# One sparse-expert layer: the products of 96-row expert jobs, alternating or in two sweeps

## The chip, the cores and the metric

The kernel runs on one core of one Trainium2 chip. The metric is the device time of one execution, in microseconds. The kernel before took 2451.39 us (median of 3 runs, 2450.69 to 2453.16).

## The reference

One layer of a diffusion backbone over 1024 latent tokens of width 1024: a mixer (a recurrent scan and a gated linear attention), a layer norm, and a mixture of experts. Only the last matters here. All in float32:

```
logits = h @ w_router + b_router            # 1024 tokens, 32 experts
top_v, top_i = top_k(logits, 4); top_w = softmax(top_v)
for the tokens xb of expert e:
    gate = min(xb @ w_gate[e] + b_gate[e], 7)
    up   = clip(xb @ w_up[e] + b_up[e], -7, 7)
    act  = (up + 1) * gate * sigmoid(1.702 * gate)
    y    = act @ w_down[e] + b_down[e]      # times the token's weight, added to its row
x = layer_norm(alpha * x + g2 * sum of y)
```

Each of the three weight matrices of an expert is 1024 x 1024 float32, 4 MB.

## The kernel before, in words

From about 797 us to 2400 us of the span the kernel works through a table of expert jobs, made on the chip. A job has one expert and at most 128 tokens. There are four kinds: 4 is full (128 rows), 3 has 96 rows, 2 has 64 rows, 1 has 32 rows. In a full job the tokens are the stationary operand of TensorE (128 columns) and the weights stream past, 512 at a time. A job of 64 rows uses half of the array's columns for each product, so two products (j = 0, 1), each over another 512 of the weight columns, lie in the two halves of the array: the "half products". A job of 32 rows has four products of 256 columns in the four quarters: the "quarter products". A job of 96 rows does both, 64 rows as half products and 32 rows as quarter products, from the same weights.

One iteration of the job loop on TensorE (in the `block.tensor` body) does, in this order: the gate and up products of job u for the first four k tiles (`gate_up(..., 0, KD // 2)`), the transposes of the activations of job u-1 (`turn`), the gate and up products for the other four k tiles, the transposes of the gathered tokens of job u+1, and the down products of job u-1 over all eight k tiles (`down`). I call these three blocks of products sections. Each section uses eight 128 x 1024 weight tiles, two in each piece: in `gate_up` k tile by k tile, first gate (g = 0), then up (g = 1); in `down` k tile by k tile. In a job of 96 rows each such tile gets two half products and then four quarter products (lines 567 to 575, and 592 to 602), so that they alternate.

Weights lie in a ring of twelve pieces of 1 MB, `ring[q]`: eight for gate and up (two k tiles each), four for down. Each has one buffer. The last product that reads a piece raises `gu_used` or `dn_used`; SyncE waits on it (`gu_pieces` at line 479, `dn_pieces` at line 507), and then issues the load of the next expert's piece into the same place. TensorE waits for a piece (`d_gu[q]`, `d_dn[q]`) before its first product with it. SyncE's queue is in order: in one iteration the eight gate and up pieces of job u+1, the two bias rows (line 513, after `gu_free`, which VectorE raises when it has read the gate and up products out of PSUM), the four down pieces of job u, and the down bias (line 509). Loads are only issued for the first job of an expert.

After the second gate/up section VectorE reads PSUM (lines 1625 and 1628) and computes the activation with ScalarE; after a down section it adds the bias and the token's weight (lines 1609, 1614), and GpSimd adds the rows to the result in DRAM with indirect DMAs (line 1758; in a job of 96 rows two, one after the other). GpSimd also gathers the tokens of later jobs (line 1745).

Of the kernel before, what the change touches and what calls it, by code (L numbers as in the profile page):

```python
# [20 lines left out]
P = 128  # L21
BANK = 512
# [15 lines left out]
def layer(nc, x, c, ctx, c_ctx, w_ada, b_ada, w_in, conv_w, conv_b, lru_wa, lru_ba, lru_wx, lru_bx,  # L38
# [7 lines left out]
    KD = D // P  # L46
# [13 lines left out]
    HT, QR = 64, 32  # L60
    QW = D // 4
# [5 lines left out]
    GUP, DNP = 8, 4  # L67
# [12 lines left out]
    with ctxs:  # L80
# [3 lines left out]
        def sem(name):  # L84
            return ctxs.enter_context(nc.semaphore(name))
# [21 lines left out]
        def reg(off, *shape):  # L107
            n = 1
            for s in shape:
                n *= s  # L110
            assert off + n <= AW
            v = arena[:, off:off + n]
            if len(shape) == 2:
                v = v.rearrange("p (a b) -> p a b", a=shape[0])
            if len(shape) == 3:
                v = v.rearrange("p (a b c) -> p a b c", a=shape[0], b=shape[1])
            if len(shape) == 4:
                v = v.rearrange("p (a b c d) -> p a b c d", a=shape[0], b=shape[1], c=shape[2])
            return v
# [104 lines left out]
        ring = [reg(2048 * q, 2, D) for q in range(GUP + DNP)]  # L224
        o = O_X1 + 8192
        xg = reg(o, D); o += 1024
        xT = reg(o, KD, P); o += 1024
# [3 lines left out]
        aT = reg(o, KD, P); o += 1024  # L231
# [10 lines left out]
        ps = [psall[:, i * BANK:(i + 1) * BANK] for i in range(8)]  # L242
# [7 lines left out]
        QUARTER_AT = {1: P - QR, 3: HT - QR}  # L250
# [40 lines left out]
        d_gu = [sem(f"d_gu{q}") for q in range(GUP)]  # L291
        d_dn = [sem(f"d_dn{q}") for q in range(DNP)]
        d_bias, d_bdn = sem("d_bias"), sem("d_bdn")
        gu_used, dn_used, gu_free = sem("gu_used"), sem("dn_used"), sem("gu_free")
# [85 lines left out]
        def settle(eng):  # L380

            eng.sem_inc(settled[eng.engine], 1)
# [167 lines left out]
        def gate_up(pe, kind, u, order_, k0, k1):  # L550
            if k0 == 0:
                pe.wait_ge(xT_ready, u + 1)
                pe.wait_ge(gu_free, u + 1)
            for k in range(k0, k1):
                for g in range(2):
                    q = 2 * (k // 2) + g
                    if k % 2 == 0:
                        pe.wait_ge(d_gu[q], order_)
                        if kind < 4:
                            settle(pe)  # L560
                    w = ring[q][:, k % 2]
                    if kind == 4:
                        for s in range(2):
                            mm = pe.matmul(ps[2 * g + s], xT[:, k, :], w[:, s * BANK:(s + 1) * BANK],  # L564
                                           start=(k == 0), stop=(k == KD - 1))
                    if kind in (2, 3):
                        for j in range(2):
                            mm = pe.matmul(ps[2 * g][HT * j:HT * j + HT, :], xT[:, k, HT:P], w[:, j * BANK:(j + 1) * BANK],  # L568
                                           start=(k == 0), stop=(k == KD - 1), skip_group_check=True)
                    if kind in (1, 3):  # L570
                        r = slice(QUARTER_AT[kind], QUARTER_AT[kind] + QR)
                        for j in range(4):
                            mm = pe.matmul(ps[2 * g + 1][QR * j:QR * j + QR, 0:QW], xT[:, k, r], w[:, j * QW:(j + 1) * QW],  # L573
                                           start=(k == 0), stop=(k == KD - 1), skip_group_check=True)
                    if k % 2:
                        mm.then_inc(gu_used, 1)

        def down(pe, kind, u, order_):
            pe.wait_ge(aT_act, u + 1)
            pe.wait_ge(aT_dve, u + 1)  # L580
            pe.wait_ge(y_biased, u + 1)
            for k in range(KD):
                if k % 2 == 0:
                    pe.wait_ge(d_dn[k // 2], order_)
                    if kind < 4:
                        settle(pe)
                w = ring[GUP + k // 2][:, k % 2]
                if kind == 4:
                    for s in range(2):
                        mm = pe.matmul(ps[6 + s], aT[:, k, :], w[:, s * BANK:(s + 1) * BANK],  # L590
                                       start=(k == 0), stop=(k == KD - 1))
                if kind in (2, 3):
                    for j in range(2):
                        mm = pe.matmul(ps[6][HT * j:HT * j + HT, :], aT[:, k % 4, HT * (k // 4):HT * (k // 4) + HT],  # L594
                                       w[:, j * BANK:(j + 1) * BANK],
                                       start=(k == 0), stop=(k == KD - 1), skip_group_check=True)
                if kind in (1, 3):
                    for j in range(4):
                        mm = pe.matmul(ps[7][QR * j:QR * j + QR, 0:QW], aT[:, 4 + k % 2, QR * (k // 2):QR * (k // 2) + QR],  # L599
                                       w[:, j * QW:(j + 1) * QW],  # L600
                                       start=(k == 0), stop=(k == KD - 1), skip_group_check=True)
                if k % 2:
                    mm.then_inc(dn_used, 1)

        def by_kind(eng, t, what):
            with eng.If(t > 2):
# [28 lines left out]
        def _(pe):  # L635
# [281 lines left out]
            with pe.Fori(0, OUTER) as o4:  # L917
                with pe.If(typ_of(pe, typ_p) + typ_of(pe, typ_c) > 0):
                    with pe.Fori(0, INNER) as i4:
                        u = o4 * INNER + i4  # L920
                        t, on_ = typ_of(pe, typ_c), ord_of(pe, ord_c, wait_c)
                        by_kind(pe, t, lambda kind: gate_up(pe, kind, u, on_, 0, KD // 2))
                        tp, op_ = typ_of(pe, typ_p), ord_of(pe, ord_p, wait_p)
                        with pe.If(tp > 0):
                            pe.wait_ge(act_ready, u + 1)
                            pe.wait_ge(xT_ready, u + 1)
                            by_kind(pe, tp, lambda kind: turn(pe, ub, JOB_KINDS[kind][2] // P, JOB_KINDS[kind][1] // P).then_inc(act_turned, 1))
                            pe.nop()
                        by_kind(pe, t, lambda kind: gate_up(pe, kind, u, on_, KD // 2, KD))
                        job_row(pe, [typ_n, ord_n], u + 2)  # L930
                        with pe.If(typ_of(pe, typ_n) > 0):
                            pe.wait_ge(xg_ready, u * 16 + 32)
                            pe.wait_ge(aT_act, u + 1)
                            pe.wait_ge(aT_dve, u + 1)
                            turn(pe, xg, KD).then_inc(x_swapped, 1)
                        by_kind(pe, tp, lambda kind: down(pe, kind, u, op_))
                        for to, of in ((typ_p, typ_c), (ord_p, ord_c), (typ_c, typ_n), (ord_c, ord_n)):
                            pe.reg_mov(to, of)
                    pe.nop()
# [892 lines left out]
```

## Time and profile before

| | |
|---|---|
| median of 3 runs | 2451.39 us |
| span of the profiled execution | 2448.2 us |
| what lies around that span, taken as the median less the span | 3.2 us |
| TensorE matmul busy | 2266.8 us, 93% of the span |
| VectorE, ScalarE, GpSimd busy | 931.4, 564.2, 230.1 us |
| DMA over the span | 567.22 MB, mean 232 GB/s |

The profiled execution has no time of its own beside its span; what is around the span is small and the same for both kernels, as far as is known. A busy TensorE is one with a matmul in flight. A group of the timeline is a run of like instructions: its start, its length until its last instruction ends, engine, line, operation and tile, and in brackets the idle time ahead of it with what ended it. TensorE's instructions overlap a little, so the true length of a group is the distance to the start of the next one. A float32 matmul of the program shows as two records.

### The profile page before, as it was taken

How to read it: one execution, taken by the hardware profiler on the slowest of the kernel's cores; microseconds unless marked ns; L12 is line 12 of the kernel's file. 1: busy time of each engine (PE TensorE's matmuls, PEld its weight loads, DVE VectorE, ACT ScalarE, POOL GpSimd, SP SyncE). 2: the span in 40 equal slices, each digit the busy share in tenths (PEclk: the TensorE clock that was granted, in tenths of full speed). 3: DMA queues.
4: the chain of work that ended last, by engine and by line, in shares of the span. 5: the costliest groups of instructions: out<-in, count | busy, mean ns of one | idle time of the engine just before them, and what ended most of it. 6: DMA issues, size and time to landing. Idle time of an engine off the chain costs nothing.

```text
span 2448.2 us, 32313 instructions
## 1 busy us (share of the span) xinstructions
PE 2266.8 (93%) x10269; PEld 1016.2 (42%) x10270; DVE 931.4 (38%) x1493; ACT 564.2 (23%) x676; POOL 230.1 (9%) x259
## 2 busy tenths in 40 slices
PE   6889999789949999999998899999999999999992
PEld 3444444554534334343442333344333444444441
DVE  2665742656661332333224232323143222222234
ACT  2333443521111122222112121212112212112113
POOL 0000000002310010010100001100001010000000
PEclk8989999889969999999999999999999999999996
DMA  9222310022245877899489999858999658997744
GB/s 332 66 79 66 101 49 26 1 85 99 95 170 210 291 275 237 299 354 380 154 306 409 375 385 404 294 176 261 342 365 397 233 175 315 311 364 265 235 122 165
DMA packets 182739, 567.22 MB, mean 232 GB/s; under 512 B 16140, under 2 KB 51136, under 8 KB 181546
## 3 DMA queue, kind: packets, MB, share of 16 engines
q1 hardware_dynamic: 167434, 524.19, 57.7%
q0 software_dynamic: 15264, 42.48, 7.1%
q8 instruction: 26, 0.43, 0.1%
q14 instruction: 15, 0.12, 0.0%
HBM read 537.26 MB, written 31.46 MB: 232 GB/s over the span
## 4 chain that ended last, share of the span: by engine, by line
PE 86%; DVE 6%; DMA 4%; SPq 1%; ACT 1%; issue 1%; POOL 0%; DVEq 0%; POOLq 0%; ACTq 0%
PE psall L564 26%; PE psall L590 13%; PE psall L568 10%; PE psall L733 10%; PE psall L573 5%; PE psall L594 5%; PE psall L631 3%; PE psall L721 3%; PE psall L844 2%; PE psall L838 2%; PE psall L599 2%; DMA arena<-in_w_down_dram 2%; PE psall L700 1%; DMA arena<-in_x_dram 1%; DVE arena L1342 1%
## 5 line engine op out<-in xcount | busy, mean ns | idle before, releaser
L564 PE MATMUL psall<-arena 128*128 128x512 f32 x1472 | 643.2, 595 | 6.8 <-DVEq L1649 3.1
L564 PEld LDWEIGHTS psall<-arena 128*128 128x128 f32 x1472 | 277.9, 191 | 350.4 <-issue 348.5
L590 PE MATMUL psall<-arena 128*128 128x512 f32 x736 | 321.8, 595 | 3.6 <-DVE arena L1662 3.6
L568 PE MATMUL psall<-arena 128*64 128x512 f32 x1152 | 280.7, 605 | 7.5 <-DMA arena<-in_w_up_dram 5.3
L1625 DVE TENSOR_TENSOR arena<-psall,arena 32x256 f32<-32x256 f32 (+2 forms) x123 | 79.9, 649 | 508.0 <-PE psall L564 321.5
L733 PE MATMUL psall<-arena 128*128 128x512 f32 (+1 forms) x608 | 246.6, 563 | 0.7 <-ACT arena L957 0.7
L1133 ACT COPY arena<-psall 128x512 f32<-128x512 f32 x49 | 28.7, 586 | 837.8 <-PE psall L631 837.8
L590 PEld LDWEIGHTS psall<-arena 128*128 128x128 f32 x736 | 138.8, 191 | 170.1 <-issue 170.1
L1609 DVE TENSOR_TENSOR arena<-psall,arena 32x256 f32<-32x256 f32 (+2 forms) x123 | 79.8, 649 | 300.6 <-PE psall L590 202.4
L1662 DVE COPY arena<-psall 128x512 f32<-128x512 f32 x49 | 33.9, 691 | 353.7 <-PE psall L631 353.6
L733 PEld LDWEIGHTS psall<-arena 128*128 128x128 f32 x608 | 116.5, 192 | 120.7 <-issue 116.4
L1136 ACT COPY arena<-psall 128x1024 f32<-128x1024 f32 x48 | 48.6, 1013 | 482.4 <-PE psall L631 482.4
L594 PE MATMUL psall<-arena 128*64 128x512 f32 x576 | 142.7, 612 | 10.8 <-DMA arena<-in_w_down_dram 10.8
L573 PE MATMUL psall<-arena 128*32 128x256 f32 x2048 | 140.3, 386 | 0.3 <-issue 0.2
L568 PEld LDWEIGHTS psall<-arena 128*64 128x64 f32 x1152 | 70.8, 136 | 148.1 <-issue 148.1
L573 PEld LDWEIGHTS psall<-arena 128*32 128x32 f32 x2048 | 52.7, 109 | 129.3 <-issue 110.8
L631 PE MATMUL psall<-ident,arena 128*128 128x128 f32 x680 | 94.0, 279 | 11.3 <-DMA arena<-h_rows,lruw 5.1
L631 PEld LDWEIGHTS psall<-ident,arena 128*128 128x128 f32 x680 | 76.8, 142 | 64.9 <-issue 59.5
L1758 POOL DMA_INDIRECT stream_rows<-arena,lruw x57 | 90.3, 1584 | 92.8 <-DMA stream_rows<-arena,lruw 45.8
L1614 DVE SCALAR_TENSOR_TENSOR arena<-arena,lruw,adarow 32x256 f32<-32x256 f32 (+2 forms) x123 | 87.0, 707 | 6.7
L1742 POOL COPY lruw<-lruw 128x1 int32 (+1 forms) x49 | 9.2, 188 | 771.8 <-PE psall L631 725.9
L1628 DVE SCALAR_TENSOR_TENSOR arena<-psall,arena 32x256 f32<-32x256 f32 (+2 forms) x123 | 79.6, 647 | 1.8
(281 smaller groups left out, 1968.2 us busy)
## 6 DMA issues: line engine op xcount, KB each, us to landing
arena<-in_w_gate_dram SPq DMA_DIRECT2D x128, 1024.0 KB, 7.1
arena<-in_w_up_dram SPq DMA_DIRECT2D x128, 1024.0 KB, 8.4
arena<-in_w_down_dram SPq DMA_DIRECT2D x128, 1024.0 KB, 7.9
arena<-in_w_ada_dram SPq DMA_DIRECT2D x16, 1024.0 KB, 5.3
arena<-in_b_gate_dram SPq DMA_DIRECT2D x32, 512.0 KB, 7.4
arena<-in_b_up_dram SPq DMA_DIRECT2D x32, 512.0 KB, 8.5
arena<-in_b_down_dram SPq DMA_DIRECT2D x32, 512.0 KB, 7.5
arena<-in_w_ada_dram SPq DMA_DIRECT2D x4, 2048.0 KB, 14.5
```

The lines of the kernel that those rows point to most:

```text
L564: mm = pe.matmul(ps[2 * g + s], xT[:, k, :], w[:, s * BANK:(s + 1) * BANK], start=(k == 0), stop=(k == KD - 1))
L568: mm = pe.matmul(ps[2 * g][HT * j:HT * j + HT, :], xT[:, k, HT:P], w[:, j * BANK:(j + 1) * BANK], start=(k == 0), stop=(k == KD - 1), skip ...
L573: mm = pe.matmul(ps[2 * g + 1][QR * j:QR * j + QR, 0:QW], xT[:, k, r], w[:, j * QW:(j + 1) * QW], start=(k == 0), stop=(k == KD - 1), skip ...
L590: mm = pe.matmul(ps[6 + s], aT[:, k, :], w[:, s * BANK:(s + 1) * BANK], start=(k == 0), stop=(k == KD - 1))
L594: mm = pe.matmul(ps[6][HT * j:HT * j + HT, :], aT[:, k % 4, HT * (k // 4):HT * (k // 4) + HT], w[:, j * BANK:(j + 1) * BANK], start=(k == ...
L631: mm = pe.transpose(psT[:, k * P:(k + 1) * P], src[:, k * P:(k + 1) * P], ident[:, :])
L733: mm = pe.matmul(ps[i % JB][0:w, 0:seg[1] - seg[0]], wring[n % WRING][:, k, 0:w], uT[:, k, seg[0]:seg[1]], start=(k == 0), stop=(k == KD - 1))
L1609: mm = dve.tensor_tensor(yb[p0:p1, c:c + n], psY[p0:p1, c:c + n], ebias[p0:p1, 2, b:b + n], ALU.add)
L1614: mm = dve.scalar_tensor_tensor(out=yb[p0:p1, c:c + n], in0=yb[p0:p1, c:c + n], scalar=(wcolq if c else wcol)[p0:p1], in1=adarow[p0:p1, 3, ...
L1625: mm = dve.tensor_tensor(gb[p0:p1, c:c + n], psG[p0:p1, c:c + n], ebias[p0:p1, 0, b:b + n], ALU.add)
L1628: mm = dve.scalar_tensor_tensor(out=ub[p0:p1, c:c + n], in0=psU[p0:p1, c:c + n], scalar=1.0, in1=ebias[p0:p1, 1, b:b + n], op0=ALU.add, op ...
L1758: return pool.indirect_dma_start(out=to, out_offset=bass.IndirectOffsetOnAxis(ap=index, axis=0), in_=yb[:, cols], in_offset=None, bounds_c ...
```

## The change

In both `gate_up` and `down` the loop over weight tiles is put inside a loop over "sweeps". A job of 96 rows has two sweeps: first all half products of the section (eight tiles, in four pieces), then all quarter products of the same tiles. Other kinds have one sweep, which is the loop as it was. The waits for pieces stand in the first sweep, the release of a piece in the last.

```diff
-            for k in range(k0, k1):
-                for g in range(2):
-                    q = 2 * (k // 2) + g
-                    if k % 2 == 0:
-                        pe.wait_ge(d_gu[q], order_)
...
-                    if kind in (2, 3):
-                        for j in range(2):
-                            mm = pe.matmul(ps[2 * g][HT * j:HT * j + HT, :], xT[:, k, HT:P], w[:, j * BANK:(j + 1) * BANK],
-                                           start=(k == 0), stop=(k == KD - 1), skip_group_check=True)
-                    if kind in (1, 3):
-                        r = slice(QUARTER_AT[kind], QUARTER_AT[kind] + QR)
-                        for j in range(4):
...
-                    if k % 2:
-                        mm.then_inc(gu_used, 1)
+            sweeps = {4: ("full",), 3: ("half", "quarter"), 2: ("half",), 1: ("quarter",)}[kind]
+            for sweep in sweeps:
+                for k in range(k0, k1):
+                    for g in range(2):
+                        q = 2 * (k // 2) + g
+                        if k % 2 == 0 and sweep == sweeps[0]:
+                            pe.wait_ge(d_gu[q], order_)
+                            if kind < 4:
+                                settle(pe)
+                        w = ring[q][:, k % 2]
...
+                        if sweep == "half":
+                            for j in range(2):
+                                mm = pe.matmul(ps[2 * g][HT * j:HT * j + HT, :], xT[:, k, HT:P], w[:, j * BANK:(j + 1) * BANK],
+                                               start=(k == 0), stop=(k == KD - 1), skip_group_check=True)
+                        if sweep == "quarter":
+                            r = slice(QUARTER_AT[kind], QUARTER_AT[kind] + QR)
+                            for j in range(4):
...
+                        if k % 2 and sweep == sweeps[-1]:
+                            mm.then_inc(gu_used, 1)
```

`down` is changed in the same way, over its eight k tiles, with `d_dn` and `dn_used`.

## Rows read from the trace of the kernel before

**Rows 1.** The page: the chain that ended last, by line.

```profile
PE psall L564 26%; PE psall L590 13%; PE psall L568 10%; PE psall L733 10%; PE psall L573 5%; PE psall L594 5%; PE psall L631 3%; PE psall L721 3%; PE psall L844 2%; PE psall L838 2%; PE psall L599 2%; DMA arena<-in_w_down_dram 2%; PE psall L700 1%; DMA arena<-in_x_dram 1%; DVE arena L1342 1%
```

**Rows 2.** Groups of instructions, page and by form: count, busy us, mean ns, idle before.

```profile
L1133 ACT COPY arena<-psall 128x512 f32<-128x512 f32 x49 | 28.7, 586 | 837.8 <-PE psall L631 837.8
...
L564 PE MATMUL psall<-arena 128*128 128x512 f32 x1472 | 643.2, 595 | 6.8 <-DVEq L1649 3.1 <-issue 1.9 <-DVE arena L1628 1.7
L568 PE MATMUL psall<-arena 128*64 128x512 f32 x1152 | 280.7, 605 | 7.5 <-DMA arena<-in_w_up_dram 5.3 <-DVE arena L1628 1.9
L573 PE MATMUL psall<-arena 128*32 128x256 f32 x2048 | 140.3, 386 | 0.3 <-issue 0.2
```

**Rows 3.** TensorE's timeline, one gate/up section of a 96-row job, start and end.

```profile
810.33 1.08 PE L568 MATMUL psall<-arena 128*64 128x512 f32 x4
811.34 0.64 PE L573 MATMUL psall<-arena 128*32 128x256 f32 x8
811.91 1.08 PE L568 MATMUL psall<-arena 128*64 128x512 f32 x4
...
822.96 1.09 PE L631 MATMUL psall<-ident,arena 128*128 128x128 f32 x8
```

**Rows 4.** TensorE's timeline where a 64-row section precedes a 32-row section.

```profile
2321.76 7.09 PE L594 MATMUL psall<-arena 128*64 128x512 f32 x32
2328.77 3.66 PE L573 MATMUL psall<-arena 128*32 128x256 f32 x64
2332.37 1.09 PE L631 MATMUL psall<-ident,arena 128*128 128x128 f32 x8
```

**Rows 5.** TensorE's waits from 797 to 2400 us: total us, times, longest.

```profile
PE psall L594 <- DMA arena<-in_w_down_dram: 10.8, 7, 2.6
PE psall L568 <- DMA arena<-in_w_up_dram: 5.3, 4, 1.7
```

**Rows 6.** Stretches: us, engines' busy us (records), TensorE clock, DMA share, GB/s.

```profile
1107.00:1170.00 63.00, 63.00 (x412) 18.29 (x412) 20.79 (x34) 13.01 (x12) 5.94 (x8) 1.00 0.98 374
1251.00:1371.00 120.00, 104.99 (x690) 36.85 (x682) 39.76 (x74) 26.02 (x24) 13.57 (x18) 1.00 1.02 394
1408.00:1563.00 155.00, 153.06 (x930) 55.59 (x918) 51.07 (x88) 30.74 (x29) 16.70 (x22) 1.00 1.01 391
1823.00:1880.00 57.00, 53.64 (x410) 19.38 (x410) 28.12 (x56) 14.25 (x13) 8.29 (x11) 0.97 1.01 389
```

**Rows 7.** Line 507 at 1142 to 1145 us: issues (first, last), us to landing.

```profile
L507 SPq DMA_DIRECT2D arena<-in_w_down_dram x4: 372/378/384, 1142.4 to 1144.3; - x4
...
DMA to landing us min/median/max: 7.3/9.2/14.1
```

**Rows 8.** The same of line 507 at 1310 to 1311 us.

```profile
L507 SPq DMA_DIRECT2D arena<-in_w_down_dram x2: 2162/2234/2305, 1307.9 to 1310.4; - x2
...
DMA to landing us min/median/max: 20.2/20.2/20.2
```

**Rows 9.** The same of line 507 at 1544 to 1545 us.

```profile
L507 SPq DMA_DIRECT2D arena<-in_w_down_dram x1: 373/373/373, 1544.4 to 1544.4; - x1
...
DMA to landing us min/median/max: 18.0/18.0/18.0
```

**Rows 10.** The same of line 479 at 1816 to 1819 us.

```profile
L479 SPq DMA_DIRECT2D arena<-in_w_gate_dram x1: 373/373/373, 1816.8 to 1816.8; - x1
...
DMA to landing us min/median/max: 5.4/6.2/6.9
```

**Rows 11.** TensorE's timeline: starts of three 96-row down sections, end of a 64-row one.

```profile
1156.93 1.08 PE L594 MATMUL psall<-arena 128*64 128x512 f32 x4
...
1321.80 1.08 PE L594 MATMUL psall<-arena 128*64 128x512 f32 x4 [1.95 <-DMA arena<-in_w_down_dram]
...
1368.24 1.94 PE L594 MATMUL psall<-arena 128*64 128x512 f32 x8 [0.58 <-DMA arena<-in_w_down_dram]
...
1560.01 1.08 PE L594 MATMUL psall<-arena 128*64 128x512 f32 x4
```

More of the change, by code:

```diff
@@ L553, in gate_up @@
                 pe.wait_ge(gu_free, u + 1)
-            for k in range(k0, k1):
-                for g in range(2):
-                    q = 2 * (k // 2) + g
-                    if k % 2 == 0:
-                        pe.wait_ge(d_gu[q], order_)
[L559 to L565, printed above, removed]
-                    if kind in (2, 3):
-                        for j in range(2):
-                            mm = pe.matmul(ps[2 * g][HT * j:HT * j + HT, :], xT[:, k, HT:P], w[:, j * BANK:(j + 1) * BANK],
-                                           start=(k == 0), stop=(k == KD - 1), skip_group_check=True)
-                    if kind in (1, 3):
-                        r = slice(QUARTER_AT[kind], QUARTER_AT[kind] + QR)
-                        for j in range(4):
-                            mm = pe.matmul(ps[2 * g + 1][QR * j:QR * j + QR, 0:QW], xT[:, k, r], w[:, j * QW:(j + 1) * QW],
-                                           start=(k == 0), stop=(k == KD - 1), skip_group_check=True)
-                    if k % 2:
-                        mm.then_inc(gu_used, 1)
@@ new lines, in gate_up @@
+            sweeps = {4: ("full",), 3: ("half", "quarter"), 2: ("half",), 1: ("quarter",)}[kind]
[8 more added lines that the diff above has]
+                        w = ring[q][:, k % 2]
+                        if sweep == "full":
+                            for s in range(2):
+                                mm = pe.matmul(ps[2 * g + s], xT[:, k, :], w[:, s * BANK:(s + 1) * BANK],
+                                               start=(k == 0), stop=(k == KD - 1))
+                        if sweep == "half":
[5 more added lines that the diff above has]
+                            for j in range(4):
+                                mm = pe.matmul(ps[2 * g + 1][QR * j:QR * j + QR, 0:QW], xT[:, k, r], w[:, j * QW:(j + 1) * QW],
+                                               start=(k == 0), stop=(k == KD - 1), skip_group_check=True)
+                        if k % 2 and sweep == sweeps[-1]:
+                            mm.then_inc(gu_used, 1)
@@ L581, in down @@
             pe.wait_ge(y_biased, u + 1)
[L582 to L603, printed above, removed]
@@ new lines, in down @@
+            sweeps = {4: ("full",), 3: ("half", "quarter"), 2: ("half",), 1: ("quarter",)}[kind]
+            for sweep in sweeps:
+                for k in range(KD):
+                    if k % 2 == 0 and sweep == sweeps[0]:
+                        pe.wait_ge(d_dn[k // 2], order_)
+                        if kind < 4:
+                            settle(pe)
+                    w = ring[GUP + k // 2][:, k % 2]
+                    if sweep == "full":
+                        for s in range(2):
+                            mm = pe.matmul(ps[6 + s], aT[:, k, :], w[:, s * BANK:(s + 1) * BANK],
+                                           start=(k == 0), stop=(k == KD - 1))
+                    if sweep == "half":
+                        for j in range(2):
+                            mm = pe.matmul(ps[6][HT * j:HT * j + HT, :], aT[:, k % 4, HT * (k // 4):HT * (k // 4) + HT],
+                                           w[:, j * BANK:(j + 1) * BANK],
+                                           start=(k == 0), stop=(k == KD - 1), skip_group_check=True)
+                    if sweep == "quarter":
+                        for j in range(4):
+                            mm = pe.matmul(ps[7][QR * j:QR * j + QR, 0:QW], aT[:, 4 + k % 2, QR * (k // 2):QR * (k // 2) + QR],
+                                           w[:, j * QW:(j + 1) * QW],
+                                           start=(k == 0), stop=(k == KD - 1), skip_group_check=True)
+                    if k % 2 and sweep == sweeps[-1]:
+                        mm.then_inc(dn_used, 1)
```

## The prediction

> **What bounds the kernel now.** I read the chain that ended last first. Nearly all of it is TensorE, and its matmuls lead line by line: the half products of lines 568 and 594 have 15% of the span, the quarter products of lines 573 and 599 have 7% [rows 1]. DMA has a small share, loads of w_down. So a shorter section of TensorE shortens the kernel, except where a weight load sets the pace. Next I read TensorE's waits in the expert stage: it waited for w_down seven times, 10.8 us in all, and for w_up four times, 5.3 us [rows 5]. That is 16 us in 1603 us, which looks like nothing. But a wait shows only where weights already come late. The third view, busy time by stretch, shows how near the others are: in four stretches that hold 96-row jobs the DMA engines are 98 to 102% busy [rows 6]. In these the loads have just enough time, and a faster TensorE can run into them. The reader is to see both: TensorE is the bound by its busy time, with a second bound close behind it in those stretches.
>
> **How many jobs and sections.** ScalarE's copy at line 1133 is run once per job, so there are 49 jobs [rows 2]. A full job has 64 gate/up records (8 k tiles, 2 matrices, 2 column blocks, 2 records each): 1472/64 = 23 full jobs. Half records: 64 per job, 1152/64 = 18 jobs of kinds 2 and 3. Quarter records: 128 per job, 2048/128 = 16 jobs of kinds 1 and 3. As 49 - 23 = 26 jobs hold halves or quarters, 18 + 16 - 26 = 8 have both. So the change touches 8 jobs of 96 rows, with 3 sections each: 24 sections. Their first gate/up sections start at about 810, 981, 1107, 1271, 1429, 1503, 1751 and 1792 us, their down sections at 867, 1032, 1157, 1322, 1490, 1560, 1819 and 1848.
>
> **What one section costs before.** A half group starts at 810.33, its quarter group at 811.34, the next half group at 811.91: 1.01 + 0.57 = 1.58 us for one weight tile. Eight of them end at 822.96: 12.63 us for the section [rows 3]. All 24 have this pattern and, within 0.2 us, this length.
>
> **What it costs after.** The two sweeps are what jobs of other kinds do already. A section of half products alone, with a quarter section behind it, takes 2328.77 - 2321.76 = 7.01 us; the quarter section, with transposes behind it, 2332.37 - 2328.77 = 3.60 us [rows 4]. Both include the changes of pattern at their ends that the new section has. Sum 10.61 us. Saved: 12.63 - 10.61 = 2.02 us per section, and 24 x 2.02 = 48.5 us if nothing else binds. The number of products, their sizes and their operands stay, so what goes is 14 of the 16 changes between halves and quarters, 2.02/14 = 0.144 us each. As rows of both patterns are there, this term has narrow ends: 1.8 to 2.1 us per section.
>
> What the trace shows here is a loss at every change of tile width. The Trainium skill ("TensorEngine Tiling (Array Packing)", Key Properties) says that changing the tiling mode drains the engine, and "TensorE: Matmul & The Clock Gate" (Step-by-step: what each phase is for) gives a drain of about 128 cycles. At 2.4 GHz this is an estimate of 0.053 us per change, 0.75 us per section and 18 us in all, against 0.144 us by the rows. I go by the rows, which are of this very work.
>
> **The waits and releases that move.** A section's four pieces were needed at 0, 1.6, 6.3 and 7.9 us (gate/up) or 0, 3.2, 6.3 and 9.5 us (down) from its start. With 7.01/8 = 0.88 us per tile in the first sweep they are needed at 0, 0.9, 3.5, 4.4 or 0, 1.75, 3.5, 5.3. Behind a late last piece come, in a down section, two tiles of halves and all quarters: 1.75 + 3.60 = 5.35 us, where it was 2 x 1.58 = 3.16. Pieces are given back in the second sweep only. For the first piece of a gate/up section that is at 7.01 + 3 x 0.45 = 8.4 us, not at 4.7; the last is given back at the section's end, 2 us earlier than before. Behind the wait on TensorE stand only TensorE's own products; behind the later release stand SyncE's loads. Where the DMA engines have a backlog, a later issue costs nothing: the loads issued at 1142.4 to 1144.3 landed up to 14.1 us later, the one at 1310.4 20.2 us later, against 5.4 us for one issued into idle engines at 1816.8 [rows 7, 8, 10]. Where they have none, the piece has a whole section or more until it is needed. So I take 0 for the later release; its end on the bad side is 3.7 us for each stretch in which loads bind, four times, 15 us; on the good side it is 0.
>
> **What the loads give back, stretch by stretch.** I take the landings in a saturated stretch as fixed by its start, since the bytes and their order stay.
>
> - Jobs at 810 and 981 (six sections): loads have gaps, landings lie several us ahead of their use. Gain 6 x 2.02 = 12.1 us.
> - Job at 1107 (98% DMA): two sections save 4.04 us, so the down section starts at 1156.93 - 4.04 = 1152.89 [rows 11]. Its last piece lands at 1144.3 + 14.1 = 1158.4 [rows 7] and is needed at 1152.89 + 5.26 = 1158.15: 0.25 us of wait. Gain 6.06 - 0.25 = 5.8 us.
> - Job at 1271: the DMA engines are full from 1251 to 1371 (102%, though TensorE is busy for only 105 of the 120 us) [rows 6], with TensorE's last wait for weights just before 1370 [rows 11]. The end of this stretch is set by the bytes alone. Gain 0. Within it the down section at 1321.80 even ends later: its last piece lands at 1310.4 + 20.2 = 1330.6 [rows 8], so its end is 1330.6 + 5.35 = 1335.95, where it was 1334.6. The next section waits for its weights in any case and takes this up.
> - Jobs at 1429 and 1503 (full from 1408 to 1563): six sections, the last at 1560.01, whose last piece lands at 1544.4 + 18.0 = 1562.4 [rows 9, 11]. Its end cannot come before 1562.4 + 5.35 = 1567.75. Before it was 1560.01 + 12.63 = 1572.64. Gain 4.9 us, not 12.1.
> - Jobs at 1751 and 1792: before 1823 loads still land 5.4 us after issue [rows 10], so they follow TensorE. The saturated part (1823 to 1880) starts with what the four gate/up sections release, thus 4 x 2.02 = 8.1 us earlier, and its end moves by the same. The two down sections in it add nothing. Gain 8.1 us.
>
> Sum: 12.1 + 5.8 + 0 + 4.9 + 8.1 = 30.9 us. The span of the profiled execution becomes 2448.2 - 30.9 = 2417.3 us; with the 3.2 us around it 2420.5 us, which stands to the median 2451.39 as before. The 16 us of waits for weights grow by what is given back, 48.5 - 30.9 = 18 us, to about 34.
>
> VectorE and GpSimd take nothing from this: VectorE reads gate and up out of PSUM in 6.3 us after a 96-row job, beside a down section that is shorter only if the job before has 96 rows too, and then still 10.6 us.
>
> **Rivals.**
>
> A. The loads never bind: in stretches above 98% the order shifts, backlogs absorb it, and all 24 sections pay. For it: only 16 us of waits now [rows 5]. Against it: the busy share of 1.01 and 1.02 leaves nothing to take [rows 6]. Then 2451.4 - 48.5 = 2402.9 us.
>
> B. The loads bind sooner than worked out: later releases open gaps in the DMA engines' work ahead of the saturated stretches (the 15 us above), and gathers and scatters of faster jobs are pulled into them. Then 2451.4 - 30.9 + 15 = 2435.5 us. The backlogs speak against it.
>
> C. Only a part of the loss at a change goes. A half group takes 1.01 us beside quarters and 0.88 alone, a quarter group 0.57 beside halves and 0.45 alone [rows 3, 4]. If the half sweep of a 96-row job kept its loss and only seven quarter groups gained, it would be 7 x 0.12 = 0.84 us per section, 24 x 0.84 = 20 us, 2431.2 us at best. Against it: the half products of a 64-row job are the same instructions on the same columns of the tokens. The skill's drain, taken alone as above, would come out near it, at 18 us.
>
> D. Slower. The mechanism is the late last piece: where each section is starved, its end is set by the landing plus the tail, and the tail grew by 5.35 - 3.16 = 2.2 us in a down section and in a gate/up section by (3 x 0.88 + 3.60) - 3 x 1.58 = 1.5 us. If all 24 are starved, 8 x 2.2 + 16 x 1.5 = 41.6 us more, 2493 us. It decides when more than half of the sections wait for their last piece. Before, one of 24 had a wait for weights (at 1321.80) [rows 11], and the wait behind it swallows the loss.
>
> E. The program does not run in the order as written, or the halves alone in a 96-row job run as before: no change, 2451 us. Nothing speaks for it; the rows of kind 2 and 1 jobs show the pure patterns.
>
> **Chances.** Forecast 0.73, A 0.09, B 0.08, C 0.05, D 0.03, E 0.02. A measurement of this kernel can tell about 0.2% (5 us) from no change. Faster: forecast, A, B and C, 0.95; same 0.02; slower 0.03. Range: 2404 (most of A) to 2435 us (B), which holds the forecast's own 2410 to 2431 and about 1 in 10 is left outside, the rest being for landings that I took as fixed.
>
> **What would show it.** In TensorE's timeline each 96-row section has one group of 32 half records, about 7.0 us, and one of 64 quarter records, about 3.6 us; no x4 and x8 alternation is left. In the groups of instructions the mean of a half record falls slightly. TensorE's waits for w_down and w_up rise from 16 to some 34 us, with new ones in the down sections that are now at 1560 and 1848, none at 867 and 1032. The DMA share of the stretch before 1370 stays at about 1. Wrong would be: a section not between 10.4 and 10.9 us where it has no wait; the time from the stretch start at 1251 to its end at 1370 getting shorter; or waits for weights in stretches with gaps in the loads.

## The result, and the profile after

The changed kernel takes 2424.79 us (median of 4 runs, 2423.19 to 2426.56), the kernel before 2451.04 us beside it: ratio 0.9892, interval [0.9877, 0.9907], 26.3 us faster. Forecast were 2420.5 us, 30.9 us faster. The span is 2423.2 us, 25.0 us shorter; of these 1.3 us lie ahead of the first 96-row section, where nothing was changed (this differs between executions by 3 us either way), and 23.2 us in the expert stage.

The chain by line on the page after. Lines 566, 570 and 575 are the gate/up products of full, half and quarter kind, 594, 598 and 603 those of down:

```profile
PE psall L566 26%; PE psall L594 13%; PE psall L737 10%; PE psall L570 9%; PE psall L575 4%; PE psall L598 4%; PE psall L635 3%; PE psall L725 3%; DMA arena<-in_w_down_dram 3%; PE psall L848 2%; PE psall L842 2%; PE psall L603 2%; SPq L479 1%; PE psall L704 1%; DMA arena<-in_x_dram 1%
```

Halves and quarters together fell from 22% to 19%; loads of w_down rose from 2% to 3% and SyncE's issue of gate/up loads has come in [rows 1]. TensorE's timeline of the first two changed sections (start, us, line) answers to [rows 3]:

```profile
809.00 7.09 PE L570 MATMUL psall<-arena 128*64 128x512 f32 x32
816.02 3.66 PE L575 MATMUL psall<-arena 128*32 128x256 f32 x64
819.61 1.09 PE L635 MATMUL psall<-ident,arena 128*128 128x128 f32 x8
```

One group of halves and one of quarters, 819.61 - 809.00 = 10.61 us, as worked out. Idle time of TensorE in the expert stage, by releaser, against [rows 5]:

```profile
PE psall L598 <- DMA arena<-in_w_down_dram: 18.6, 15, 2.9
PE psall L570 <- DMA arena<-in_w_up_dram: 9.4, 7, 2.0
...
PE psall L575 <- DMA arena<-in_w_up_dram: 3.2, 2, 1.9
...
PE psall L575 <- DMA arena<-in_w_gate_dram: 1.1, 1, 1.1
```

Waits for weights are 18.6 + 9.4 + 3.2 + 1.1 = 32.3 us, where they were 16.1. How this is spread tells more than the sum. I call lead the time by which a section starts earlier than the same section in the kernel before (both by TensorE's timeline), and list by how much it grows in each stretch; the times are those of the kernel before.

| lead gained, us | 810-1170 | 1170-1370 | 1370-1573 | 1573-1737 | 1737-1923 | 1923-2391 | stage |
|---|---|---|---|---|---|---|---|
| forecast | 17.9 | 0 | 4.9 | 0 | 8.1 | 0 | 30.9 |
| changed kernel | 17.8 | 0.0 | 4.6 | -0.2 | 1.2 | -0.2 | 23.2 |
| the same, second profile (e11) | 17.7 | 0.0 | 3.4 | -0.2 | 1.2 | -0.2 | 21.8 |

In the first profile three stretches came out within 0.3 us of the forecast; in the second the third of them is 1.5 us short. The last stretch with 96-row jobs brought 1.2 us in both where 8.1 were forecast, and that is nearly the whole difference.

### The profile page after: what moved, and what is told of

Its sections match the earlier page's. It is cut to its first block, busy times and chain, and to the rows that moved or that the text cites. A ratio compares the mean times of both kernels' runs of the same rounds, so it can differ in the third digit from the quotient of the medians.

```text
span 2423.2 us, 32313 instructions
## 1 busy us (share of the span) xinstructions
PE 2222.8 (92%) x10269; PEld 1051.2 (43%) x10270; DVE 931.1 (38%) x1493; ACT 564.2 (23%) x676; POOL 230.9 (10%) x259
## 4 chain that ended last, share of the span: by engine, by line
PE 83%; DVE 6%; DMA 5%; SPq 3%; issue 1%; ACT 1%; POOL 0%; DVEq 0%; POOLq 0%; ACTq 0%
PE psall L566 26%; PE psall L594 13%; PE psall L737 10%; PE psall L570 9%; PE psall L575 4%; PE psall L598 4%; PE psall L635 3%; PE psall L725 3%; DMA arena<-in_w_down_dram 3%; PE psall L848 2%; PE psall L842 2%; PE psall L603 2%; SPq L479 1%; PE psall L704 1%; DMA arena<-in_x_dram 1%
## 5 line engine op out<-in xcount | busy, mean ns | idle before, releaser
L570 PE MATMUL psall<-arena 128*64 128x512 f32 x1152 | 258.3, 598 | 12.9 <-DMA arena<-in_w_up_dram 9.4
L570 PEld LDWEIGHTS psall<-arena 128*64 128x64 f32 x1152 | 83.4, 137 | 170.7 <-issue 170.7
L598 PE MATMUL psall<-arena 128*64 128x512 f32 x576 | 130.8, 599 | 18.6 <-DMA arena<-in_w_down_dram 18.6
L575 PE MATMUL psall<-arena 128*32 128x256 f32 x2048 | 119.1, 384 | 5.0 <-DMA arena<-in_w_up_dram 3.2
L575 PEld LDWEIGHTS psall<-arena 128*32 128x32 f32 x2048 | 64.4, 110 | 63.8 <-issue 27.1
L598 PEld LDWEIGHTS psall<-arena 128*64 128x64 f32 x576 | 40.2, 136 | 95.9 <-issue 95.7
```

## Experiments

Time ratios are against the kernel before on the same chip; leads are as above.

**Half the bytes (e3, e4).** The edit, on each of the two orders, for gate/up (down likewise):

```diff
-                    sp.dma_start(ring[q], w_v[ds(e, 1)].rearrange("a p c n -> p (a c) n")).then_inc(d_gu[q], 16)
+                    n_ = D if u is None else D // 2
+                    sp.dma_start(ring[q][:, :, 0:n_], w_v[ds(e, 1)].rearrange("a p c n -> p (a c) n")[:, :, 0:n_]).then_inc(d_gu[q], 16)
```

> The old order, with each weight load after the first expert's bringing only the first half of its columns (half the bytes; the products read what lies there, so the values of the experts differ). Theory: in the old order weights cost 16 us of waits on TensorE and nothing else, so the time falls by 12 to 18 us, to about 2435 us, and the waits for weights are gone. Rival (the loads also slow TensorE in other ways, in SBUF or by their issue): the time falls by more than 20 us.

> The two sweeps, with the same half loads. Theory: a 96-row section saves 2.02 us and what is lacking of 24 x 2.02 = 48.5 us in the changed kernel (about 23 us) was given back to the weight loads. Then this one is 45 to 49 us faster than the half loads in the old order, about 2388 us. Rival (part of the saving is lost on TensorE or its queue itself, by the waits, the sections' ends, or VectorE's release of PSUM): the difference between the two is 25 to 40 us, and idle time before matmuls shows other causes than DMA.

Measured: old order 2429.15 us, 0.9919 [0.9903, 0.9934]; two sweeps 2383.82 us, 0.9742 [0.9726, 0.9757]. No wait for weights is left in either. The first is 20 us below the kernel before, at the rival's edge; its lead shows where: 15.0 us from 1170 to 1370 and 5.5 us from 1737 to 1923, nowhere else, against 16.1 us of waits. The pair differs by 45.3 us, by the leads 44.2 us. So with the loads out of the way the change is worth nearly what 24 sections promise, and in the true kernel 21 of these 44 us went back to the loads. The missing 4.3 us of 48.5 are another matter: the eight second gate/up sections save 1.80 to 1.87 us in place of 2.02, five of the down sections 1.3 to 1.8. TensorE's timeline of e4 behind such a down section:

```profile
869.25 3.66 PE L604 MATMUL psall<-arena 128*32 128x256 f32 x64
873.42 1.10 PE L567 MATMUL psall<-arena 128*128 128x512 f32 x2 [0.52 <-issue]
```

The quarter group takes 4.17 us to the next start, not 3.60, and the idle time has no releaser but "issue".

**Quarters first (e9)**, with half loads:

```diff
-            sweeps = {4: ("full",), 3: ("half", "quarter"), 2: ("half",), 1: ("quarter",)}[kind]
+            sweeps = {4: ("full",), 3: ("quarter", "half"), 2: ("half",), 1: ("quarter",)}[kind]
```

> Two sweeps with the quarter products first, so that a section ends in half products; half loads as in e4, so no load binds. With halves first, the half-load pair gained 44 us in place of 48.5: a section followed by transposes or by another kind's products took 10.8 to 11.4 us in place of 10.6. Theory that TensorE's queue has nothing in stock after a run of short products (64 records of 0.056 us) and its branch shows: with halves last the ends are covered as in the old order, all sections take 10.6 us, and the gain over the old order with half loads is 47 to 49 us, 3 to 4 us faster than e4. Rival (the ends cost the same whatever stands last, by the drain of the array): no faster than e4, within 1 us.

Measured: 2381.54 us, 0.9720 [0.9697, 0.9742], in time not told apart from e4. The timeline does tell them apart. The same section in e9:

```profile
862.37 3.66 PE L604 MATMUL psall<-arena 128*32 128x256 f32 x64
865.96 7.09 PE L599 MATMUL psall<-arena 128*64 128x512 f32 x32
872.97 1.55 PE L567 MATMUL psall<-arena 128*128 128x512 f32 x3
```

It takes 10.60 us with no idle time behind it, and every 96-row section of e9 takes 10.50 to 10.62. By the leads e9 gains 48.0 us over e3, the 48.5 of the sum. So the ends of sections cost 4 us when short products stand last. That it is TensorE's queue that has run out fits the name of the idle time, but only the order was tried.

**One part alone (e1, e2).** `gate_up` or `down` of the changed kernel put into the one before.

> Two sweeps in gate_up only, down in the old order. 16 sections x 2.02 = 32.3 us gross. Theory: leads by stretch (against the old kernel) 12.1 us from the jobs at 810, 981 and 1107, 0 at 1271, 7.1 us from 1429 to 1573 (the last down section ends 3.16 us after its last piece lands, not 5.35), 1 us from 1751 to 1882: 20 us, about 2431 us. Rival (a stretch gives what TensorE saves): 28 us or more.

> Two sweeps in down only. 8 sections x 2.02 = 16.2 us gross. Theory that the stretch 1740 to 1882 was already filled by its loads: 6.1 (three jobs) + 0 + 4.0 (1490, 1560) + 1 (1819, 1848) = 11 us, about 2440 us. Theory that late releases of gate/up pieces eat the gain there: those are as before here, so 4.0 for the last stretch, 14 us, about 2437 us; TensorE's lead over the old kernel at its end (the full job at 1882) tells it, 1 or 4 us more than ahead of 1751.

Measured: gate/up alone 2426.76 us, 0.9909 [0.9896, 0.9923]; down alone 2441.32 us, 0.9971 [0.9961, 0.9980]. In the stretch 1737 to 1923 the lead grew by 4.7 us with gate/up alone and by -0.9 us with down alone, against 1.2 us with both. Neither theory had this: a stretch full by its loads would have given 1 us to each, late gate/up releases 4 us to down. The stretch has room for some 5 us, and two sweeps in down take it away. In time, gate/up alone is not told apart from both together (0.9892 and, in e11, 0.9900), though it has two thirds of the saving on TensorE. From 1370 to 1573 gate/up alone gained 4.8 us, where I expected 7.1.

**Late releases alone (e7).** The old alternation, with the pieces of a 96-row section released by its last weight tile(s), in down likewise:

```diff
+                            if kind == 3 and k == k1 - 1 and (2 * g + j // 2, j % 2) in ((0, 1), (1, 1), (2, 1), (3, 1)):
+                                mm.then_inc(gu_used, 1)
-                    if k % 2:
+                    if k % 2 and kind != 3:
                         mm.then_inc(gu_used, 1)
```

> The old alternation; only the release of the pieces of a 96-row section is put off to its last weight tile(s): the first gate/up piece comes free at 10.8 us of 12.6, where it was 4.7 (8.4 of 10.6 with two sweeps). TensorE's work is unchanged. Theory that the late releases took the gain from 1751 to 1882: the end of that stretch comes 3 us or more later than in the old kernel, time 2453 to 2457. Theory that its loads were at their limit in any case and the late last piece and its tail took it: late releases cost at most 1.5 us there, time within 2 us of the old one.

Measured: 2450.67 us, 1.0004 [0.9996, 1.0013]: no cost that the time shows. The leads are 1.3 us in the first stretch (a wait ahead of transposes at 1031 is gone, which comes and goes with such shifts), 0 in the other four, and -2.2 us from 1737 to 1923. So late releases do cost there, more than the 1.5 us that I allowed and less than 3. They open gaps: in the 26 us from 1751 on the DMA share was 1.02 before and is 0.80 in the same part of e7.

**No quarters in 96-row jobs (e5)**, old order:

```diff
-                    if kind in (1, 3):
+                    if kind == 1:
                         r = slice(QUARTER_AT[kind], QUARTER_AT[kind] + QR)
```

> The old order without the quarter products of 96-row jobs (a third of their rows is left out). A section is 7.0 us, pieces come free at once: 24 x 5.6 = 134 us gross. Theory that loads set the pace from about 1740 to 1882: TensorE's lead over the old kernel grows there by no more than 6 us, though the six sections in it have 33 us less work; 0 from 1271 to 1370, at most 10 from 1429 to 1573, about 45 from the three first jobs: time 2385 to 2400. Theory of the late releases: with none, the lead in that stretch grows by 15 us or more, time under 2380.

Measured: 2399.48 us, 0.9797 [0.9783, 0.9812]. This gives the room of each stretch, as TensorE has far less to do and pieces come free at once: 42.5, 0.1, 6.4 and 4.7 us. The start of the full job's products at 1737 and of those at 1923 (before: 1737.19 and 1923.40), in e5:

```profile
1687.48 2.31 PE L590 MATMUL psall<-arena 128*128 128x512 f32 x5
...
1869.00 2.31 PE L590 MATMUL psall<-arena 128*128 128x512 f32 x5
```

181.52 us, before 186.21: 4.7 us less for 33 us less work. That stretch is bound by its loads, with some 5 us of room and not 8.

**Shorter sweeps (e6, e8).** In e6 a section is cut in two, with both sweeps over each half; in e8 only a down section is.

```diff
-            for sweep in sweeps:
-                for k in range(k0, k1):
+            step = 2 if kind == 3 else k1 - k0
+            for c0, sweep in [(c, sw) for c in range(k0, k1, step) for sw in sweeps]:
+                for k in range(c0, c0 + step):
```

> Two sweeps over half a section, then two over the other half: 12 of 16 changes of width go in place of 14, so 2.02 - 0.29 = 1.73 us per section where loads don't bind, 41.5 us gross. The tail behind a late last piece is (0.88 + 0.88) + 1.8 = 3.6 us in a down section, not 5.35, and half of the pieces come free at mid-section. Theory that tail and release cost what the changed kernel lacks beyond the limit of the loads: leads in the stretches with gaps 1.7 to 2.6 us less than the two sweeps, from 1429 to 1573 and 1751 to 1882 together 3 to 5 us more: 2421 to 2424 us. Theory that only the bytes count: 2427 us, slower than the two sweeps.

> Whole sweeps in gate/up, two half-section ones in down. Against the changed kernel: 8 down sections lose 0.29 us each where no load binds (six of them, 1.7 us), and the tail behind a late last piece is 3.6 us, not 5.35. Gate/up only gained as much in the stretch 1751 to 1882 as it had room for (its lead grew by 4.7 us, with down swept by 1.2 us). Theory of the tail: the stretches 1429 to 1573 and 1751 to 1882 gain 1.7 us each at least, 2420 to 2423 us. Rival (the order in down does not matter there): 2426 us.

Measured: e6 2422.65 us, 0.9892 [0.9878, 0.9907]; e8 2422.27 us, 0.9888 [0.9874, 0.9902]. As times neither is told apart from the changed kernel. The leads are: e6 15.0, 0.0, 5.8, 4.9 us from 1737 to 1923; e8 17.3, -0.1, 5.6, 3.6 us. Down in two halves gives 2.4 us back in the disputed stretch, gate/up in two halves as well another 1.3, and there e6 reaches the room. From 1370 to 1573 e8 gained 1.1 us more than the changed kernel (2.3 more than e11), not the 1.7 expected.

**Mirrored (e10), beside the changed kernel again (e11), and with half loads (e12).** The order of a 96-row section:

```diff
+                     3: [("half", k0, mid), ("quarter", k0, mid), ("quarter", mid, k1), ("half", mid, k1)]}[kind]
```

> Full loads. A 96-row section in the order halves, quarters for its first two pieces, quarters, halves for the other two: two changes of width inside it, one more than with two sweeps, half of the pieces free at mid-section, halves at the end, and a tail behind a late last piece in a down section of 0.9 + 3.5 = 4.4 us, not 5.35. Theory: 2.02 - 0.14 = 1.88 us a section, the ends covered (about 3 us back), and leads from 1429 to 1573 and 1751 to 1882 at least those of e6: 2419 to 2422 us. Rival (ends don't matter): like e6, 2422 to 2425 us.

> The changed kernel once more, beside e10 on one chip: 2423 to 2427 us, by either theory.

> The mirrored order with half loads. Two more changes of width than none: 12.63 - 10.61 - 0.14 = 1.88 us a section, 24 x 1.88 = 45 us over the old order with half loads if the ends are covered by the halves, about 1 us faster than e4. If the ends are not covered, 41 us, 3 us slower than e4.

Measured: e10 2426.10 us, 0.9898 [0.9882, 0.9915], e11 2426.98 us, 0.9900 [0.9885, 0.9915]: the same time. The leads of e10 are 16.4, -0.2, 4.6 and 5.2 us, 25.6 us in the stage against 21.8 in e11, but runs differ by as much ahead of the stage. I had expected to see this version win, and the time does not show it. e12 took 2387.53 us, 0.9740 [0.9719, 0.9761]; its sections take 10.66 to 10.76 us as expected, yet by the leads it gains 42.9 us over e3 and not 45. Of the missing 2 us, 1.7 are the clock: behind 1.9 us of idle time a full gate/up section that starts at 1421.11 takes 15.5 us, where the same one took 13.8 in e3, at a granted clock of 0.67 from 1421 to 1425 and 0.90 in the next 4 us; in e3 the clock was at 1.00 in this section, though it stands behind the same 1.9 us of idle time. What decides between the two is not shown.

## Why the prediction was right or wrong

**The price of a section: right.** 12.63 us became 10.61. With no loads in the way and the ends covered, 24 sections gave 48.0 us (e9), forecast 48.5. Rows of jobs that already ran the pure patterns were a sound source [rows 4]. The estimate of 18 us, worked out from the drain of about 128 cycles that the Trainium skill gives ("TensorE: Matmul & The Clock Gate", Step-by-step: what each phase is for), is too small by more than half: the runs show 0.144 us per change, not 0.053. The shorter sweeps agree: a section with two changes more takes 10.89 us (e6), with one more 10.76 (e10), against 10.61.

**The ends of sections: a term left out.** I took 3.60 us for a quarter group from one place. In other places it is 3.8 to 4.4 us, and with halves first it is not (e9). In the first three jobs the nine sections gave 17.0 us in place of 18.2 gross. A wait of 1.2 us ahead of transposes at 1031 that went away hid it, while 0.5 us were lost at 1074 and the 0.25 us of wait at 1157 did not come: 17.8 against 17.9 us is in part luck. By my own sign of being wrong (a section outside 10.4 to 10.9 us without a wait) this term had failed: the down sections at 867, 1819 and 1848 took 11.2, 11.5 and 11.1 us and waited for no weights.

**The stretch before 1370: right, to the 0.0.** Six us of saved products came to nothing. Even e5 with 17 us less work gained 0.1.

**The late last piece and its tail: right for this kernel, but not the whole rule.** In the down section at 1560, now at 1534.69 (changed kernel, TensorE's timeline):

```profile
1534.69 1.94 PE L598 MATMUL psall<-arena 128*64 128x512 f32 x8 [1.41 <-DMA arena<-in_w_down_dram]
...
1543.51 1.94 PE L598 MATMUL psall<-arena 128*64 128x512 f32 x8 [1.56 <-DMA arena<-in_w_down_dram]
1545.38 3.66 PE L603 MATMUL psall<-arena 128*32 128x256 f32 x64
1548.98 1.54 PE L566 MATMUL psall<-arena 128*128 128x512 f32 x3
```

From the start of the last piece's products to the end are 1548.98 - 1543.51 = 5.47 us, forecast 5.35, and the stretch gained 4.6 us, forecast 4.9. But e1, with the short tail in down, gained only 4.8 there. Its alternating section waited 1.4 us for its first piece, and 12.63 us behind that it ended 0.3 us ahead of the changed kernel's. So the longer tail costs 0.3 us here and not 2.2, because the first landing held the old order nearly as long. In e11 the stretch gained 3.4: the granted clock was 0.50 to 0.71 for 8 us ahead of this section, and its last piece came into use 1.2 us later.

**The step that failed: "before 1823 loads still land 5.4 us after issue, so they follow TensorE", hence 8.1 us.** A short time from issue to landing says that no backlog stands, not that the DMA engines have time to spare. Stretches of the kernel before and the changed one, in the columns of [rows 6]:

```profile
1740.00:1882.00 142.00, 138.64 (x915) 46.02 (x914) 50.02 (x89) 28.07 (x26) 15.26 (x20) 0.99 1.01 378
```

```profile
1727.00:1751.00 24.00, 23.91 (x211) 10.35 (x210) 4.19 (x5) 1.87 (x2) 1.77 (x2) 1.00 0.96 346
1751.00:1856.00 105.00, 93.45 (x681) 39.10 (x680) 43.56 (x83) 24.15 (x22) 14.05 (x18) 0.98 1.03 400
```

The engines were 101% busy over all 142 us before, from 1740 on and not from 1823, and 98% in the 4 us around the load at 1816.8, which I had called one into idle engines. In the changed kernel they have gaps at its start (96%), where pieces are released in a bunch at the ends of sections, and then are full for 105 us. The runs put this in the place of 8.1 us: 3.4 us were never to be had, as the room is about 5 us (4.7 in e5; e1, e6 and e10 reached 4.7, 4.9 and 5.2).

The other 3.5 us were lost behind the 96-row jobs. None of the six 96-row sections of this stretch waits for weights in the changed kernel, so the grown tail has no part in it. The last waits stand in the down section of the 64-row job behind them, and a full gate/up section follows. The last piece and that section, in the changed kernel and then in its second profile, e11:

```profile
1853.39 2.52 PE L598 MATMUL psall<-arena 128*64 128x512 f32 x8 [2.94 <-DMA arena<-in_w_down_dram]
1855.85 15.06 PE L566 MATMUL psall<-arena 128*128 128x512 f32 x32
```

```profile
1854.77 3.38 PE L598 MATMUL psall<-arena 128*64 128x512 f32 x8 [3.18 <-DMA arena<-in_w_down_dram]
1858.08 14.00 PE L566 MATMUL psall<-arena 128*128 128x512 f32 x32
```

Counted from the start of the stretch (the full down section at 1737), this piece came into use at 142.6 us before, 139.7 in the changed kernel, 140.0 in e11, 139.0 in e8, 137.7 in e6 and 137.9 in e5. So late loads take 1.8 us of the 3.5 (2.1 in e11). Late release, which I had priced at 0 with 3.7 us per stretch as its bad end, has a part in this: e7 lost 2.2 us to a stronger one alone. It is not all, since e1 has the same gaps (96% in the same 24 us) and lost nothing. Between 110 and 140 us of the stretch GpSimd's DMA queue, with the gathers and row adds, moved 1.37 MB in the changed kernel, 1.01 in e1 and 0.90 before. At 400 GB/s the 0.36 MB more than in e1 are an estimate of 0.9 us; no run tried this alone. e6 and e10 moved as much there (1.29 and 1.38 MB), but SyncE's queue, with the weights, had moved 0.5 and 0.8 MB more by 110 us.

The rest, 1.7 us, is the clock. The last piece's products took 2.46 us, where they took 1.87 before, and the section from 1855.85 took 14.9 us, where it was 13.8. In e11 the products took 3.31 us and the section 13.8: 1.4 us. The clock (last column but two) in two stretches of 4 us:

```profile
1850.00:1854.00 4.00, 1.06 (x7) 0.38 (x6) 0.00 (x0) 0.00 (x0) 0.00 (x0) 1.00 1.03 414
1854.00:1858.00 4.00, 4.00 (x11) 1.31 (x7) 1.91 (x3) 0.00 (x0) 0.00 (x0) 0.58 1.03 416
```

TensorE was busy for 1 of 4 us, and in the next 4 us its mean granted clock was 0.58, that is mostly at the lower of the levels 1.2 and 2.4 GHz. Before, the clock fell too (0.61 from 1872 to 1876), but ahead of the wait for the last piece, which took it up; the last piece's products and the full section ran at 1.00.

**The rivals.** A (all 24 sections pay) is what e9 does with half loads; in the true kernel it is excluded by the room of 0.1, 6.4 and 4.7 us in three stretches. B was right in kind (gaps opened by late releases, and perhaps the gathers and row adds) in one stretch of four, at about 2 us in place of 15. D's mechanism, the grown tail, acts in the down sections at 1322 and 1560 only, and its condition (more than half of the sections starved) is far off. 32.3 us of waits for weights against 34 forecast is near in part by luck: by the same rule (16 us and what is given back) the 25.3 us that were given back would make 41. The ends of sections, the clock, and waits that are longer than their rows hold the rest. The waits forecast for the 96-row down section at 1848 came one down section later. C and E are excluded by the sections of 10.61 us.

## What to carry to other kernels

When a bound engine is made faster, work out for each stretch how much time the next resource leaves. The time from issue to landing tells a backlog, not spare time: by it I forecast 8.1 us. The busy share over the whole stretch comes nearer, but is no exact measure either: at 1.01 it promised about 1 us (so I expected in e1), and 5 were to be had; with pieces released at once the same engines moved 397 GB/s over the first 110 us of this stretch (e5), against 370 before. Grouping products by tile width pays what rows of the pure patterns say, but it moves the first use of every buffer forward and its release back; with loads in the way, groups half as long reached the room in the tight stretch (e6) at no more time in all. Count also where TensorE's clock stands behind the last wait. Leads of marked sections between two traces locate a gain of 1 us that run times, which spread by 1 to 10 us here, can't; but take two traces of a kernel, since two of the changed kernel differ by 1.2 us in one stretch.

## What the runs showed of the hardware

- A change between 64-column and 32-column products costs TensorE 0.144 us (2.02 us for 14 of them, e9 and [rows 3, 4]; 0.28 us for two, e6; 0.15 for one, e10). Changes of PSUM bank within a run of halves cost nothing to be seen: 32 half records take 7.02 us in gate/up, where two banks alternate, and 7.01 in down, which has one.
- Behind 64 short product records (0.056 us each) TensorE loses 0.2 to 0.8 us at the end of 13 of the 24 sections; behind long ones it loses none (e4 against e9).
- Half the weight bytes make the old order 20 us faster, though its rows of waits for weights sum to 16 us. From 1170 to 1370 the lead of e3 is 15.0 us for 12.9 us of such waits, at a granted clock of 1.00 throughout: each of the nine waits costs some 0.2 us more than its row shows. That a row of idle time starts at the modelled end of a matmul fits this, but was not tested. From 1737 to 1923 it is 5.5 us for 3.2, and there TensorE also fell to a mean clock of 0.61 in the 4 us from 1872, behind a wait.
- The granted clock fell behind idle time of TensorE. Where no wait stood behind the fall, it cost 1.7 us in the changed kernel (1.4 in e11) and 1.7 in e12; before, a fall stood ahead of a wait for weights (clock 0.61 from 1872 to 1876), and the landing set the end all the same.
